# Joint ACT tables for logarithm and exponential, and Pool's quarter sums of the input at the layer's start

## What is computed

```python
h = rmsnorm(x, norm_g) * (1 + scale) + shift        # scale, shift, gate from a conditioning vector
proj = h @ w_in                                     # split into 16 parts
# branch a, RWKV-7, 8 heads, two directions
kk = k * k_k; kk = kk / max(sqrt(sum(kk * kk)), 1e-12)
decay = exp(-exp(-softplus(-(w0 + tanh(wd) @ w2)) - 0.5)); a = sigmoid(a0 + ad @ a2)
o_a = group_norm(scan(r, decay, k, v, kk, a)) + bonus
# branch b, gated linear attention (GLA), 4 heads, two directions
g = log_sigmoid(gad @ a2 + ab) / 16
o_b = rmsnorm(chunk_scan(q, k, v, g), norm_g)
# branch c, latent attention (MLA), 8 heads
q = rmsnorm(qd, qn_g) @ wq_up; ckv = rmsnorm(kvd, kvn_g)
o_c = softmax attention over own tokens and cached context
y = sum over branches of sigmoid(merge) * ((o * silu(g)) @ out)
x = x + gate * (y @ w_out)
```

## Time and profile before

| | |
|---|---|
| timed runs | 2651.58, 2652.35, 2657.53 us, median 2652.35 us |
| profiled execution | 2648.37 us, span of its instructions 2646.6 us |
| mean granted TensorE clock | 0.991 |
| TensorE busy | 2520.8 us |
| DVE busy | 1368.0 us |
| ACT busy | 920.9 us |
| Pool busy | 291.4 us |

### The profile page before, as it was taken

The page is one execution under the profiler, slowest core; times in us unless marked ns, Lnnn a source line. Parts: engine busy times, 40 slices in busy tenths (PEclk is TensorE's granted clock), DMA queues, the critical chain, the costliest instruction groups (busy, mean ns, idle before and its releaser), DMA issues.

```text
span 2646.6 us, 50148 instructions
## 1 busy us (share of the span) xinstructions
PE 2520.8 (95%) x21400; PEld 1751.2 (66%) x21400; DVE 1368.0 (52%) x2641; ACT 920.9 (35%) x1524; POOL 291.4 (11%) x290
## 2 busy tenths in 40 slices
PE   7999999999999999999999999999999999999997
PEld 3675857667566666677656767585866666666764
DVE  3554536364577555443436465554638755453443
ACT  3424324142454544212024242423325545432211
POOL 0100000000000211333401000000000020123432
PEclk9999999999999999999999999999999999999998
DMA  7102020211201100222411010101000010012222
GB/s 284 41 23 85 10 91 26 76 40 40 69 25 37 52 17 27 72 72 71 138 58 33 10 43 2 51 2 35 18 27 33 25 56 17 19 56 70 66 78 71
DMA packets 35690, 136.50 MB, mean 52 GB/s; under 512 B 4624, under 2 KB 4784, under 8 KB 34576
## 3 DMA queue, kind: packets, MB, share of 16 engines
q1 hardware_dynamic: 31392, 116.35, 12.7%
q0 software_dynamic: 4080, 16.94, 1.9%
HBM read 126.30 MB, written 6.98 MB: 50 GB/s over the span
## 4 chain that ended last, share of the span: by engine, by line
PE 82%; DVE 9%; ACT 6%; issue 2%; DMA 1%; POOL 0%; SPq 0%; ACTq 0%; DVEq 0%; POOLq 0%
PE psum L665 80%; PE psum L668 2%; DVE tmp L1635 2%; DVE tmp L1638 1%; DVE tmp L2170 1%; DVE acts L1635 1%; ACT tmp L1584 1%; DVE tmp L1646 1%; ACT tmp L1321 1%; DMA ring<-units 1%; ACT L1316 0%; ACT L1312 0%; DVE acts L1638 0%; DVE tmp L2055 0%; ACT L1484 0%
## 5 line engine op out<-in xcount | busy, mean ns | idle before, releaser
L665 PE MATMUL psum<-hT,ring 128*128 128x512 f32 (+2 forms) x3024 | 877.5, 441 | 8.3 <-DVE hT L1643 4.9
L665 PE MATMUL psum<-tmp 64*64 64x64 f32 (+9 forms) x10624 | 703.2, 258 | 42.3 <-DVE tmp L1638 10.4
L665 PEld LDWEIGHTS psum<-hT,ring 128*128 128x128 f32 x3024 | 492.8, 191 | 376.9 <-issue 318.3
L665 PEld LDWEIGHTS psum<-tmp 64*64 64x64 f32 (+3 forms) x10624 | 553.3, 149 | 160.4 <-issue 59.3
L1321 ACT ACTIVATE tmp<-psum 128x256 f32<-128x256 f32 (+8 forms) x562 | 284.2, 508 | 912.7 <-PE psum L665 835.6
L1635 DVE TENSOR_TENSOR tmp<-tmp,psum 128x320 f32<-128x320 f32 x240 | 112.7, 486 | 309.1 <-PE psum L665 268.2
L1321 ACT ACTIVATE acts<-psum 128x256 f32<-128x256 f32 (+5 forms) x212 | 108.9, 513 | 270.6 <-PE psum L665 247.9
L1635 DVE TENSOR_TENSOR tmp<-psum,tmp 128x256 f32<-128x256 f32 (+2 forms) x184 | 75.7, 411 | 232.6 <-PE psum L665 207.1
L1635 DVE TENSOR_TENSOR tmp<-tmp 128x320 f32<-128x320 f32 (+2 forms) x214 | 136.6, 665 | 5.6
L600 POOL DMA_DIRECT2D new_rw<-tmp x8 | 4.5, 563 | 1082.0 <-DVE tmp L1926 1082.0
L1638 DVE TENSOR_TENSOR tmp<-tmp 128x640 f32<-128x640 f32 (+1 forms) x128 | 94.0, 755 | 57.1 <-ACT tmp L1316 32.6
(11 more groups left out here) (179 smaller groups left out, 2610.5 us busy)
## 6 DMA issues: line engine op xcount, KB each, us to landing
ring<-units SPq DMA_DIRECT2D x210, 512.0 KB, 3.5
hT<-xT SPq DMA_DIRECT2D x2, 1280.0 KB, 7.1
tmp<-xT POOLq DMA_DIRECT2D x8, 320.0 KB, 3.9
x_keep<-hT POOLq DMA_DIRECT2D x8, 320.0 KB, 4.1
tmp<-x_keep POOLq DMA_DIRECT2D x8, 320.0 KB, 3.2
yT<-acts POOLq DMA_DIRECT2D x8, 320.0 KB, 3.2
tmp<-late POOLq DMA_DIRECT2D x2, 1024.0 KB, 7.7
tmp<-masks SPq DMA_DIRECT2D x1, 1408.0 KB, 11.7
```

The lines of the kernel that those rows point to most:

```text
L665: return nc.tensor.matmul(out, lhsT, rhs, start=start, stop=stop, skip_group_check=True)
```

## The change

It has two parts. On Pool, the sums of the input's quarters wait for the 16 signals that the eight tiles of the layer's normalised input are done, instead of for a bank of pair 0. On ACT, sets of tables are named in the code. The set `natural_log_exp_and_others` holds logarithm and exponential; it is loaded ahead of the wait of every root and ahead of the wait of a gate's logarithm. The set `natural_log` is loaded ahead of the logarithm of kk, and `exp_and_others` (exponential and tanh) behind the roots of q and kv.

```diff
                 b12 = hT[:, 0:4, HT:T]
-                pool.wait_ge(filled.sem, filled[("X", l, 0, 0)])
+                for k in range(KT):
+                    pool.wait_ge(act_h.sem, act_h[l, k])
+                    pool.wait_ge(dve_h.sem, dve_h[l, k])
                 nc.gpsimd.tensor_tensor(h_parts["t3"], h_parts["22"], b12, ALU.subtract).then_inc(pool_ht.sem, pool_ht.mark(l, "t3"))
...
+            def logs_and_exponentials():
+
+                nc.scalar.preload_act_table_set("natural_log_exp_and_others")
+
+            def exponentials():
+
+                nc.scalar.preload_act_table_set("exp_and_others")
+
             def rstd(key, out, scale, eps):
 
+                if key[0] in ('goss', 'xss', 'qss', 'kvss', 'ovar'):
+                    logs_and_exponentials()
                 act.wait_ge(filled.sem, filled[key])
...
                 for p in range(PAIRS):
                     project(l, BESIDE[p][0])
 
+                    nc.scalar.preload_act_table_set("natural_log")
                     act.wait_ge(dve_e.sem, dve_e[("kkss", l, p)])
...
                 def gla_log(p, d):
 
+                    logs_and_exponentials()
                     act.wait_ge(dve_gax.sem, dve_gax[l, p, d])
...
                 rstd(("kvss", l), m_r[1], 1.0 / 128, 0).then_inc(act_kvrs.sem, act_kvrs.mark(l))
+                exponentials()
                 copies(l, MA[0], items(MA[0]), "254")
```

## The result

| | before | after |
|---|---|---|
| timed runs beside each other | 2651.58 to 2657.76, median 2654.94 us | 2623.58, 2623.77, 2623.91, 2630.9, median 2623.84 us |
| ratio, 95% interval | | 0.989 [0.9867, 0.9912] |
| profiled execution | 2648.37 us, span 2646.6, clock 0.991 | 2630.9 us, span 2629.1, clock 0.992 |

The kernel became 1.1% faster; 2629 was forecast, within 2618 to 2641. The two profiled executions are 17.5 us apart, the medians 31 us. The profiled execution of after is the longest of its four runs and has a granted clock of 0.992, where the other three have 0.995. So the profiles show the parts of the change, and a good part of the median's gain has to be looked for in the clock.

A forecast was written before the change was run, and what follows sets the result against it. TensorE, busy 95% of the span, was taken as the bound, so only its idle time counts. Pool 9.9, norms 2.6, GLA 7.8 and clock 3.3 sum to 23.6 us: from 2652.35 to 2629 us, range 2618 to 2641.

The forecast's parts named there:

- Pool's part: Pair 0 of both RWKV layers: its excess of 4.46 and 5.42 us goes, 9.9 us; sums beside DVE's memsets cost nothing.
- The two norms: Start of layer 1 and end of program: the second table load, 1.28 us each, goes; 2.6 us, bounds 0 and 2.6.
- GLA: GLA part of both layers: fewer exposed table loads shorten TensorE's idle times, 3.9 us per layer, 7.8 in all.
- the gates: GLA gates: logarithm and sigmoid come 0.9 us earlier, saving 0.9 us of TensorE idle time at each of two turns.
- the roots: GLA heads, each layer: four loads become two; 1.5 us at the attention products, 0.7 us at the head of MLA.
- DVE's run into the state products: GLA, first two heads: level exponential comes 2.6 us earlier, but TensorE's state products limit the gain to 1.5 us.
- the 0.1 lost: First GLA gate of each layer: its table load only moves, with 0.1 us lost.
- The clock: GLA attention products in layer 1: TensorE's clock stays high behind the shortened idle time; 3.3 us, bounds 0 and 3.3.
- (1): Rival: ACT's part gives nothing in GLA, as DVE's or TensorE's work ends each wait, and the clock falls; 2640, chance 0.14.
- (2): Rival: Pool's collision only moves, and what it meets at the layer's start is late by as much; 2639 us, chance 0.05.
- (4): Rival: slower, named table loads come on top of those standing now, 16.2 us in both layers; 2658.7 us, chance 0.04.
- (3): Rival: TensorE's clock falls elsewhere as work behind pair 0 shifts; two more falls 2635.5, two fewer 2622.3 us; chance 0.19.

## Why the prediction was right, and where it was too small

**Pool's part** (9.9 us): the place, the cause and the cost at the new place were as said. 9.5 us were measured by medians. But the 9.9 taken from the length of a stretch are not all waiting: about 6.4 us are idle time of TensorE (2.72 and 3.65), and 3.4 us the low clock behind it, in the profiled execution of before already. The prediction didn't see that this term held clock, and counted a clock term for GLA alone.

**The two norms** (2.6 us): 2.5 +- 1.0 measured, 1.28 us each in the rows.

**GLA** (7.8 us): ACT's part less the norms is 10.9 - 2.5 = 8.4 us at one clock. Undone one by one, the gates are worth 3.7 +- 1.5 (forecast 2 x 1.8 = 3.6) and the roots 5.8 +- 1.5 (forecast 2 x 2.2 = 4.4; the idle times in their profile are 2 x 2.1), or 2.9 and 5.0 with a constant for each chip. DVE's run into the state products came as worked out: 1.44 us of the 2.56 reach TensorE. At the first gate 3.04 us of DVE's wait became 3.18, the 0.1 lost.

**The clock** (3.3 us): this is the term that was mis-sized. Its mechanism was right: a shorter idle time of TensorE, and no fall behind it. But it was priced by the one fall that the profile of before showed in GLA. The mean clock of the runs goes from 0.9898 to 0.9941, and 0.0043 at 2.15 us for 0.001 is 9.2 us; by the profiles' own falls it is 10 or 11. The forecast had 3.3 us and, unseen, 3.4 in Pool's term, 6.7 in all. A fall costs 1.7 or 3.4 us in these windows, and the same idle time has one in one execution and none in the next, so that one profile is a poor price for it; the count over several executions, as seven of eight against none of eighteen, tells it.

So the sum stands thus: 23.6 us were forecast, and 28.2 measured, the difference of the means of all runs, 2653.5 and 2625.3. Without the clock 9.9 - 3.4 + 2.6 + 7.8 = 16.9 us were forecast, against 19.0 +- 1.3 by the fit and 17.0 or 18.2 by the profiles; the rest, 9 to 11 us where 6.7 were forecast, is clock. Of the 4.6 us that the forecast lacked, 2.5 to 4.5 are thus clock. Whether an edit gave more than its rows say, by up to 2 us, isn't settled.

**The rivals.** (1) fell with the gates and the roots as before. (2) fell by the memsets' 5.35 us. (4) fell by the 21 loads fewer; but what it rests on is partly so, since ten of the loads named are of the set that was active and were paid all the same, and two of them, at the first gates, are worth 2.2 us by the trace. (3) was the nearest to what happened: fewer falls, with the time that it gave for that, 2622.3, among the measured runs. The reason given for it, work that shifts, isn't the one that the counts point to; the falls went where the idle times went.

That the runs differ by clock is shown by their list; that the idle time causes the fall is argued from its place ahead of each fall and from the counts, and no run here changed an idle time of TensorE and nothing else.

## What to carry to other kernels

Where TensorE is busy nearly all the time, price a wait by the idle time that it leaves on TensorE, and look at the granted clock in the windows behind it: stalls of 1.15 us and more had a fall behind them here that took 1.7 or 3.4 us of clock, in some executions and not in others. Compare programs at one clock before saying which edit gave what; here 9 to 11 of 28 us were clock. An operation on Pool did no harm where DVE had a pause or cleared scratch, and a table load that was named where the set was already active was paid all the same.

## What the runs showed of the hardware that was not expected

- A DVE copy of 128x5 elements, with one operand in SBUF, was held for 2.68 us by a Pool sum, while memsets weren't held at all (5.35 us). The Trainium skill's "SBUF — State Buffer", section "Who interferes with whom", counts copies among the operations that can take the ports shared with Pool, and says that the one that issues first has them for its whole instruction. The trace agrees with both: the copy of 92.05 us ends 0.02 us after Pool's third sum, at 94.73.
- The hold goes both ways. DVE's product of 87.09 us, begun 0.04 us before Pool's second sum, kept its 0.82 us, and that sum took 3.53 instead of 2.90; the third took 3.96, behind the scan.
- On one core alone, with nothing beside it, the runs of one program spread over 14.7 us (before, 2647.0 to 2661.71), and a mean clock between 0.992 and 0.986 accounts for three quarters of their variance.
- Idle times of 1.35 us between softmax products had no fall of the clock behind them in any of the thirteen profiles (0 of 52 places), while shorter ones of 1.15 us in GLA had one in 13 of 26. Late in layer 0, behind idle times of 1.49 and 1.86 us that the change doesn't touch, it fell in 12 of 13 profiles.
